# The output product of a decoder step: half of its features computed with the activations as TensorE weights

## What the kernel computes

```
y  = x + gate[:, None] * (u @ w_out)          # u: (tokens, 1024), w_out: (1024, 1024)
                                              # gate: one row of 1024 for the prompt, one for each of 8 samples
out = y * rsqrt(mean(y * y, axis=-1) + 1e-6) * final_g
```

## Time and profile before

| | |
|---|---|
| median of three runs | 756.62 us |
| the profiled execution | 757.0 us |
| its span, first to last instruction | 755.3 us |
| mean granted TensorE clock | 0.949 |
| TensorE matmul busy | 688.0 us, 91% |
| ScalarE, VectorE, GpSimd busy | 45%, 64%, 61% |

### The profile page before, as it was taken

The page is one execution under the profiler, slowest core; times in us unless marked ns, Lnnn a source line. Parts: engine busy times, 40 slices in busy tenths (PEclk is TensorE's granted clock), DMA queues, the critical chain, the costliest instruction groups (busy, mean ns, idle before and its releaser), DMA issues.

```text
span 755.3 us, 14932 instructions
## 1 busy us (share of the span) xinstructions
PE 688.0 (91%) x5066; PEld 618.9 (82%) x5066; DVE 482.8 (64%) x468; ACT 338.2 (45%) x760; POOL 464.3 (61%) x293
## 2 busy tenths in 40 slices
PE   2899999998988889999999999995899999999992
PEld 0576888786867858988999999985889998999992
DVE  0530589898988975895696597667665369343222
ACT  5634474646353335454463563530422225233554
POOL 4211266685756515898789679666594656666651
PEclk9898899999989979999999999999699999999996
DMA  8976858988788761277866768659247365832102
GB/s 315 336 253 220 243 174 249 272 252 271 237 269 265 215 207 29 87 237 208 250 199 185 216 208 241 182 177 240 56 122 212 97 181 154 266 85 83 57 0 113
DMA packets 156904, 144.71 MB, mean 192 GB/s; under 512 B 7547, under 2 KB 115152, under 8 KB 156852
## 3 DMA queue, kind: packets, MB, share of 16 engines
q1 hardware_dynamic: 142696, 136.10, 60.0%
q10 hardware_dynamic: 14164, 8.07, 3.4%
HBM read 135.10 MB, written 9.11 MB: 191 GB/s over the span
## 4 chain that ended last, share of the span: by engine, by line
PE 33%; issue 23%; POOL 20%; DVE 11%; SPq 6%; DMA 4%; ACT 1%; POOLq 0%; DVEq 0%; ACTq 0%
PE ps L545 26%; POOL sb_wL L1417 8%; POOL sb_arenaA L1491 8%; POOL sb_arenaA L1459 3%; DMA sb_arenaA<-in_w_ada 3%; DVE sb_arenaA L1728 2%; SPq L392 2%; SPq L393 2%; DVE sb_arenaA L1870 1%; PE ps L579 1%; DVE sb_arenaA L1875 1%; DVE sb_arenaB L1875 1%; DVE sb_arenaA L1732 1%; PE ps L653 1%; PE ps L900 1%
## 5 line engine op out<-in xcount | busy, mean ns | idle before, releaser
L1417 POOL TENSOR_TENSOR sb_wL<-sb_wraw,sb_wH 128x512 fp32r<-128x512 f32 (+1 forms) x176 | 236.3, 1359 | 200.0 <-ACT sb_wH L960 183.7
L545 PE MATMUL ps<-sb_hH,sb_wH 128*128 128x260 f32 x1152 | 241.6, 292 | 1.6 <-ACT sb_arenaB L965 0.9
L545 PE MATMUL ps<-sb_hL,sb_wH 128*128 128x260 f32 x1152 | 235.5, 287 | 0.0
L545 PE MATMUL ps<-sb_hH,sb_wL 128*128 128x260 f32 x1152 | 235.1, 286 | 0.0
L545 PEld LDWEIGHTS ps<-sb_hH,sb_wH 128*128 128x128 f32 x1152 | 181.7, 193 | 14.9 <-issue 10.6
L960 ACT ACTIVATE sb_wH<-sb_wraw 128x512 fp32r<-128x512 f32 (+1 forms) x176 | 104.1, 613 | 195.0 <-PE ps L545 158.6
L545 PEld LDWEIGHTS ps<-sb_hL,sb_wH 128*128 128x128 f32 x1152 | 181.6, 193 | 0.0
L545 PEld LDWEIGHTS ps<-sb_hH,sb_wL 128*128 128x128 f32 x1152 | 181.2, 192 | 0.0
L1491 POOL TENSOR_TENSOR sb_arenaA<-sb_arenaA 128x2048 f32<-128x2048 f32 x32 | 116.0, 3631 | 5.0 <-DMA sb_arenaA<-in_cache_v 3.0
L1732 DVE TENSOR_REDUCE sb_arenaA<-sb_arenaA 128x2048 f32 (+1 forms) x32 | 72.9, 2284 | 4.4 <-DVE sb_arenaA L1728 2.5
L1459 POOL TENSOR_TENSOR sb_arenaA<-sb_arenaA 128x2048 f32<-128x2048 f32 x11 | 54.3, 4939 | 29.5 <-DMA sb_arenaA<-in_cache_k 29.5
(11 more groups left out here) (356 smaller groups left out, 949.9 us busy)
## 6 DMA issues: line engine op xcount, KB each, us to landing
sb_wraw<-in_w_in SPq DMA_DIRECT2D x64, 512.0 KB, 5.2
sb_arenaA<-in_cache_k SPq DMA_DIRECT2D x128, 256.0 KB, 3.1
sb_arenaA<-in_cache_v SPq DMA_DIRECT2D x128, 256.0 KB, 3.3
sb_arenaA<-in_w_ada SPq DMA_DIRECT2D x6, 2048.0 KB, 12.4
sb_arenaB<-in_state_C SPq DMA_DIRECT2D x8, 512.0 KB, 3.9
sb_wraw<-in_w_mlstm SPq DMA_DIRECT2D x8, 512.0 KB, 4.4
sb_wraw<-in_w_out SPq DMA_DIRECT2D x8, 512.0 KB, 3.7
sb_arenaB<-in_x_prompt SPq DMA_DIRECT2D x1, 2048.0 KB
```

Source lines behind the costliest of these rows:

```text
L545: last = mm(ps[:, 2 * s + a, 0:HALF], w[:, s, k, :], x[:, k, a * HALF:(a + 1) * HALF], start=(k == 0 and w is wH and x is xH), stop=(k == ...
L1417: tt(wL[:, j % 2, part], wraw[:, j % 4, part], wH[:, j % 2, part].bitcast(F32), ALU.subtract)\
```

## The change

Tiles T_OUT to T_OUT + 3 (features 0 to 511) stay as they are, with their turns. Features 512 to 1023 of the prompt are computed the other way round. `hH` and `hL`, which are free once the `w_mlstm` product is done, take the high and low parts of w_out's last four tiles as 8 x 128 rows of 512 columns (`wide_high` on ScalarE, `wide_low` on VectorE). `out_tokens(i)` then uses 128 tokens of u as the stationary operand and streams 512 columns of w_out: 8 x 3 = 24 matmuls for a block of 128 tokens and 512 features, already in tokens by features, in PSUM bank i.

The gate is now along the columns, so it is needed as a row that all partitions hold (`alphaB`) and as 8 rows for the samples (`alphaS`). TensorE makes both ahead of the `w_mlstm` product and ScalarE copies them. VectorE multiplies the block in PSUM by `alphaB` and adds it to x (`added`). The samples' last 512 features come from eight small matmuls in plain float32 in four column groups (`uS`, 32 wide, with the raw w_out) and one that adds the groups. Squares, root, scaling and store are made for each token block by itself (`token_squares`, `deviation`, `finish`, `token_scale`): VectorE scales the second 512 features and ScalarE the first, and all five stores are issued from SP's queue.

```diff
@@ sync
-            for i, j in enumerate((0, 2)):
+            for i, what in enumerate((0, 1, None, 2, 3)):
                 sp.wait_ge(y_rdy, i + 1)
-                sp.dma_start(y_rows[:, j, :], yN[:, j, :]).then_inc(st_y, 16)
-            sp.wait_ge(y_rdy, 3)
-            sp.dma_start(O["y_s"].rearrange("b o d -> (b o) d"), ysN).then_inc(st_y, 16)
+                if what is None:
+                    sp.dma_start(O["y_s"].rearrange("b o d -> (b o) d"), ysN).then_inc(st_y, 16)
+                else:
+                    sp.wait_ge(y_act, what + 1)
+                    sp.dma_start(y_rows[:, what, :], yN[:, what, :]).then_inc(st_y, 16)
@@ tensor
             pe.wait_ge(ym_lo, 3)
+            pe.wait_ge(mod_rdy, 3)
+            pe.wait_ge(kq_used, 2 + 8)
+            for j in range(4):
+                mm(ps[:, 6, j * P:(j + 1) * P], modT[:, 20 + j, B:B + 1].broadcast_to([P, P]), ident[:, :],
+                   start=True, stop=True)
+            for j in range(4):
+                last = tr(ps[0:B, 7, j * P:(j + 1) * P], modT[:, 20 + j, 0:B], ident[:, :])
+            last.then_inc(fin_pe, 1)
...
+            out_turn(0, 0)
+            ztile(2, T_OUT + 2, uH, uL)
+            out_turn(1, 1)
+            ztile(3, T_OUT + 3, uH, uL)
+            out_turn(0, 2)
+
+            def out_tokens(i):
+                pe.wait_ge(z_free, T_OUT + (5 if i < 2 else 6))
+                for k in range(KT):
+                    for u, w in ((uH, hH), (uH, hL), (uL, hH)):
+                        last = mm(ps[:, i, :], u[:, k, i * P:(i + 1) * P], w[:, k, 0:D // 2],
+                                  start=(k == 0 and u is uH and w is hH), stop=(k == KT - 1 and u is uL))
+                last.then_inc(ot_mm, 1)
+
+            pe.wait_ge(kq_lo, 1 + 4)
+            out_tokens(0)
+            out_turn(1, 3)
+            pe.wait_ge(y_acc, 2 + 3)
+            for k in range(KT):
+                g = k % 4
+                last = mm(ps[32 * g:32 * g + 32, 4, :], uS[:, k, :], wraw[:, :, k, :], start=(k < 4), stop=(k >= 4))
+            last.then_inc(fin_pe, 1)
+            out_tokens(1)
+            pe.wait_ge(fin_act, 4)
+            mm(ps[0:B, 5, :], groupsum[:, 0:B], groups, start=True, stop=True).then_inc(ot_mm, 1)
+            out_tokens(2)
+            out_tokens(3)
@@ scalar
+            act.wait_ge(fin_pe, 2)
+            f(alphaB, ps[:, 6, :], ACT.Copy).then_inc(fin_act, 1)
+            f(alphaS, ps[0:B, 7, :], ACT.Copy).then_inc(fin_act, 1)
...
+            def wide_high(j):
+                act.wait_ge(ld_w[j % 4], 16 * (T_OUT // 4 + 2))
+                act.wait_ge(z_done, T_OUT + 2)
+                f(hH[:, :, (j - 4) * P:(j - 3) * P], wraw[:, j % 4], ACT.Copy).then_inc(ym_hi, 1)
...
+            def token_squares(i, acc):
+                act.wait_ge(y_acc, acc)
+                chain(f(osq[:, 0:D // 2], xN[:, i, D // 2:D], ACT.Square, accum_out=ssq[:, 4, i:i + 1]))
+
+            def token_scale(i, var):
+                act.wait_ge(y_var, var)
+                f(yN[:, i, 0:D // 2], yN[:, i, 0:D // 2], ACT.Copy, scale=ssq[:, 5, i:i + 1]).then_inc(y_act, 1)
...
@@ gpsimd
-            for j in range(8):
-                if j < 6:
-                    low(j + 2, T_OUT + j + 2)
-                if j >= 1:
-                    gained(j - 1)
-            gained(KT - 1)
+            for j in range(2):
+                low(j + 2, T_OUT + j + 2)
+            for j in range(4):
+                gained(j)
@@ vector
+            def wide_low(j):
+                dve.wait_ge(ym_hi, 2 + j - 3)
+                col = slice((j - 4) * P, (j - 3) * P)
+                tt(hL[:, :, col], wraw[:, j % 4], hH[:, :, col].bitcast(F32), ALU.subtract).then_inc(kq_lo, 1)
...
+            def added(x, acc, alpha, count):
+                dve.wait_ge(ot_mm, count)
+                chain(tt(acc, acc, alpha, ALU.mult))
+                tt(x[:, second], x[:, second], acc, ALU.add).then_inc(y_acc, 1)
+
+            def finish(i, number, std, whole=False):
+                rows = B if whole else P
+                x, y = (xs2, ysN) if whole else (xN[:, i], yN[:, i])
+                dve.wait_ge(y_acc, number)
+                chain(tt(y[:, second], x[:, second], fg[0:rows, second], ALU.mult))
+                dve.wait_ge(y_std, std)
+                v.reciprocal(ssq[0:rows, 5, i:i + 1], rstd[0:rows, i:i + 1]).then_inc(y_var, 1)
+                dve.wait_ge(y_var, 1 + std)
+                part = slice(0, D) if whole else second
+                v.tensor_scalar(y[:, part], y[:, part], ssq[0:rows, 5, i:i + 1], None, ALU.mult).then_inc(y_rdy, 1)
...
```

More of the change, by code:

```diff
@@ L1385, in _, with deviation @@
-            squares(KT - 1)
-            act.wait_ge(y_var, 1)
[L1387 to L1394, removed]
+            def deviation(i, rows):
+                f(rstd[0:rows, i:i + 1], ssq[0:rows, 4, i:i + 1], ACT.Sqrt, scale=1.0 / D, bias=ss[0:rows, i:i + 1])\
+                    .then_inc(y_std, 1)
@@ new lines, in token_squares @@
+            def token_squares(i, acc):
[4 more added lines that the diff above has]
+                f(yN[:, i, 0:D // 2], yN[:, i, 0:D // 2], ACT.Copy, scale=ssq[:, 5, i:i + 1]).then_inc(y_act, 1)
+            wide_high(4)
+            wide_high(5)
+            high(2, T_OUT + 2, T_OUT // 4)
+            out_leave(0)
@@ new lines, in _ @@
+            high(3, T_OUT + 3, T_OUT // 4)
+            out_leave(1)
+            squares(0)
+            wide_high(6)
+            out_leave(2)
+            wide_high(7)
+            squares(1)
+            out_leave(3)
+            squares(2)
+            token_squares(0, 6)
+            squares(3)
+            act.wait_ge(y_var, 1)
+            deviation(0, P)
+            act.wait_ge(y_gain, 4)
+            token_scale(0, 2)
+            act.wait_ge(fin_pe, 3)
+            f(groups, ps[:, 4, :], ACT.Copy).then_inc(fin_act, 1)
@@ L1396, in _ @@
+            token_squares(1, 8)
+            deviation(1, P)
+            token_scale(1, 3)
+            act.wait_ge(y_acc, 9)
+            chain(f(osq[0:B, 0:D // 2], xs2[:, D // 2:D], ACT.Square, accum_out=ssq[0:B, 4, 4:5]))
+            deviation(4, B)
+            for i in (2, 3):
+                token_squares(i, 8 + i)
+                deviation(i, P)
+                token_scale(i, 3 + i)
             act.wait_ge(st_misc, 16 * 6)
@@ L2062, in _ @@
             chain(v.memset(ssq, 0.0))
+            dve.wait_ge(uu_rdy, 1 + KT)
+            v.tensor_copy(uS[:, :, 0:B], sgm[:, :, T:NT])
             dve.wait_ge(ld_xo, 48)
[L2064 to L2070, removed]
@@ L2079, in _, with token_added @@
-            v.tensor_scalar(ysN, ysN, ss[0:B, 4:5], None, ALU.mult).then_inc(y_rdy, 1)
+            wide_low(4)
+            wide_low(5)
+            gated_sample(0)
+            turned(0, 1)
+            gated_sample(1)
+            wide_low(6)
+            turned(1, 2)
+            gated_sample(2)
+            wide_low(7)
+            turned(2, 3)
+            gated_sample(3)
+            dve.wait_ge(fin_act, 3)
+            def token_added(i, count):
+                added(xN[:, i], ps[:, i, :], alphaB, count)
@@ new lines, in _ @@
+            token_added(0, 4)
+            turned(3, 5)
+            dve.wait_ge(y_sq, 4)
+            chain(v.tensor_reduce(rstd[:, :], ssq[:, 0:4].rearrange("p c j -> p j c"), AX, ALU.add))
+            v.tensor_scalar(ss[:, :], rstd[:, :], 1.0 / D, EPS, ALU.mult, ALU.add).then_inc(y_var, 1)
+            finish(0, 6, 1)
+            token_added(1, 6)
+            finish(1, 8, 2)
+            added(xs2, ps[0:B, 5, :], alphaS, 7)
+            dve.wait_ge(y_gain, 4)
+            finish(4, 9, 3, True)
```

68 lines of the change are left out of this document (33 added, 35 removed).

## The result

The changed kernel takes 747.13 us (median of 9 runs, 743.70 to 750.10) against 756.16 us of the kernel before (9 runs, 750.60 to 757.75): a ratio of 0.9903, 95% interval 0.9876 to 0.9930, faster by 5.3 to 9.4 us. I forecast 751.5 us, in a range of 749.3 to 754.3.

The account below looks back on a forecast made before the run. TensorE, busy until 739.81 us, and a 15.5 us tail were taken to bound the kernel. TensorE +3.2 and tail -8.3 took 5.1 us off the span of 755.3; median forecast 751.5 us, range 749.3 to 754.3.

Parts of the forecast that it names:

- gate rows: TensorE ahead of the w_mlstm product: four matmuls and four transposes add 1.4 us, between 1.2 and 1.9.
- four tiles and three turns replaced: TensorE's w_out product: 24.6 us of tiles and turns become 26.4 us in the changed program, 1.8 more.
- tail: From the last product's end to the end of the span: from 15.5 to 7.2 us, -8.3.
- The level: Base of the forecast: profiled execution 757.0 us, 0.4 above the median of 756.62, less 5.1, gives a median of 751.5.
- 512-column streams at 0.235 us: Token blocks on TensorE: 96 matmuls at 0.235 us take 22.6 us, against 23.0 for the four tiles.
- The cheaper stream of 0.216: Rival: 512-column matmuls run at 0.216 us as in plain float32, giving 749.7 us; 8 in 100.
- The slower rival: Token blocks: weight loads not hidden under the 512-column stream; halfway, 9.6 us more, 761 us; 4 in 100.
- Changes of shape, 0.5 us: TensorE's w_out product: four changes of shape or operand cost 0.5 us in all, between 0 and 0.7.
- No helper late: Wide pieces and groups' copy come before TensorE wants them, thinnest cover 0.8 us; late-helper rival 1 to 3 us, 14 in 100.
- The tail's steps, 3.5 us to the last issue: Behind token block 3: gate product, addition, square, root, reciprocal and scaling take 3.5 us with gaps; last store issued at 746.5.
- The lone store: End of span: last 512 KB store takes 3.7 us from issue, bounds 3.3 and 5.8; long-store rival +2.1 us, 6 in 100.

Follow-up runs that it names:

- the one large store: Kernel before with only the last of its four 512 KB stores and the small one, three token blocks not written: stretch 117.72 us, tail 12.64 us.
- the held stores: Changed kernel with all five stores held back until the last token block is scaled: stretch 120.32 us, ratio to the kernel before 0.9984.
- before again: The kernel before run once more with no edit: median 755.41 us of 12 runs, ratio 1.0018 to the kernel before, stretch 120.53 us.

## Why the prediction was right and wrong

What a run can show step by step is the stretch. Forecast and measured, us:

| term | forecast | measured |
|---|---|---|
| gate rows | +1.4 | +1.03 (the edit alone, and its removal 1.0) |
| four tiles and three turns replaced | +1.8 | +1.36 |
| tail | -8.3 | -8.80 |
| sum | -5.1 | -6.4 |

- **The level.** The step that failed is the base of the forecast: "this execution lies 0.4 above the median of 756.62, so the forecast for the median is 751.5 us". I took three runs as the kernel's level and the range as that of the edit alone. Runs of one kernel spread over 6 to 11 us. Of the nine runs of the kernel before that stand beside the result, the three that I had are among the four slowest, and the other six have their median at 752.5; 35 later runs have theirs at 753.3, 13 at 753.8 and 12 at 755.4. My 1.5 us for what a measurement can tell from no change was too small as well: nine runs against nine left 2 us to either side. Taking the measured 6.4 us off 756.6 gives 750.2, inside the range; taking it off 753.3 gives 746.9, within 0.3 us of what was measured, and below the range. My own 5.1 off 753.3 would have been 748.2, also below. A miss of the level alone was enough for the time to leave the range, and the terms together moved it a further 1.3.
- **512-column streams at 0.235 us**: 0.2315, so 96 of them take 22.2 us and not 22.6, and the swap by itself gives 0.8 us against the four tiles' 23.0. The cheaper stream of 0.216, the rival for which the Trainium skill ("TensorE: Matmul & The Clock Gate", "Back-to-back issue gap") also stood, did not come; that section calls its formula the isolated gap and has 131 ns for 512 columns in a sustained stream, and no run here shows that either. The slower rival, weight loads that don't hide, did not come: 48 loads instead of 24 a block cost 0.1 us.
- **Changes of shape, 0.5 us**: about that. Blocks, turn and samples add up to 26.0 us from 709.30 to 735.30, against 26.4. Without the streams' 22.2, the turn's 0.55, the samples' 1.85 and the sum of the groups' 0.96 some 0.4 us are left for the changes and for the end of the last matmul.
- **The gate rows**: they take 0.92 + 0.44 = 1.36 us, as I said, but part of that was a gap before: TensorE stood 0.2 us at the start of the w_mlstm product, and the first new instruction fills it. How the rest of the 0.3 splits was not tried.
- **No helper late**: right, TensorE does not wait once in the w_out product. The copy of the groups ended at 721.98 us, 1.0 ahead of its use (I said 0.8).
- **The tail's steps, 3.5 us to the last issue**: 3.6. The root took 0.29 instead of 0.21 and the square was exact.
- **The lone store**: 3.7 us allowed, 3.0 measured from SP's queue and 3.4 from ScalarE's. This term was mis-sized by 0.7, the largest error in the sum of the edit. "to landing" in the earlier trace rows counts from the issue for loads and stores of other shapes, and I put 0.3 on top of it.
- **What the tail was made of**: I read it as squares. Ahead of the prediction I even counted 16 of 128 columns behind the last product; the trace has eight, of tiles 6 and 7, and one of the samples for each. Leaving them out was worth 1.4 us; behind them stood GpSimd's product with `final_g`, with which VectorE's next step collides. The change took both away, since that product of the last half now runs on VectorE beside ScalarE's square. The tail's sum came out nearly right all the same, since I priced the new steps one by one; the cause of the old ones I had only half seen. The stores' queueing was 2.4 us and an issue between two scalings 0.4 (shown by the one large store), and the issues on one queue are another 2.6 that a changed kernel without the early stores would have paid (shown by the held stores).

The profiles differ by another 6.9 us ahead of the product of squares. Over all twelve profiles it lies between 627.7 and 635.1 us, both of these in a kernel with one small edit in its last part, and the two kernels' own four stand at 634.7 and 630.9, 627.8 and 630.4. By the order of VectorE's operations nearly all of the difference between the first two profiles arises between 226 and 287 us, where the sums over cached pages end and the choice of blocks is made. The largest step in it is one addition: ahead of it the changed kernel leads by 2.2 us, behind it by 6.6. Before:

```profile
237.30 4.59 POOL L1459 TENSOR_TENSOR sb_arenaA<-sb_arenaA 128x2048 f32<-128x2048 f32 x1 [4.58 <-DMA sb_arenaA<-in_cache_k]
237.34 6.70 DVE L1728 TENSOR_TENSOR sb_arenaA<-sb_arenaA 128x2048 f32<-128x2048 f32 x1
```

After:

```profile
235.13 2.28 DVE L1800 TENSOR_TENSOR sb_arenaA<-sb_arenaA 128x2048 f32<-128x2048 f32 x1
235.26 6.64 POOL L1533 TENSOR_TENSOR sb_arenaA<-sb_arenaA 128x2048 f32<-128x2048 f32 x1 [4.70 <-DMA sb_arenaA<-in_cache_k]
```

Two additions of 2048 columns meet. The one that starts second, VectorE's by 0.04 us or GpSimd's by 0.13, takes 4.4 us longer or 2.1. It is the collision of the kernel's tail again, and an order settled by a tenth of a microsecond moves VectorE by 4.4 us. Six of the twelve profiles, with edits of either kernel among them, have VectorE's addition long at this place (5.2 to 6.7 us instead of 2.28). It is not the whole of the scatter: the lead is down to 5.0 us at 254 us and back to 7.1 at 287, two other profiles, the latest of all among them, have such an addition at 195 us instead, and what settles the order was not tried. The fall of TensorE's clock behind the wait for VectorE, seen in two of twelve profiles at 1.2 to 1.5 us each, is a second, smaller source. In the timed runs, too, a slower one tends to have the lower mean granted clock (before again: 751.32 us at 0.962, 760.30 at 0.947); which of the two follows from the other was not tried.

## What to carry to other kernels

When TensorE is busy to the end, swapping which operand is stationary gives it little (0.8 us here, less than the gate rows and the samples cost); what pays is that a product's last piece leaves in the layout and the portion in which it can be finished and stored, so that norm, scaling and stores of all other pieces run beside TensorE. Price a tail by everything in it: the late engine, the one right behind it, the issues in one queue and the bytes in flight. And before a range is given, ask how far runs of the same kernel spread: a change of under 1% is read from a stretch of the trace between two fixed instructions. Here it repeated to 0.01 us, except where the granted clock fell in it, while the median of three runs was 3 us off.

## What the runs showed of the hardware beyond this

- A 512-column fp32r matmul costs 0.2315 us at full clock and a 256-column one 0.118: 0.44 ns a column and about 5 ns fixed. A pass of plain float32 comes to 0.216 us for 512 columns, so the fp32r form costs more for each pass.
- A VectorE operation of 5 columns took 1.60 instead of 0.17 us and one of 8 columns 0.68 instead of 0.15, each ending with a GpSimd operation with two SBUF inputs. Of two additions of 2048 columns that met, the second to start took 6.6 to 6.7 us.
- The last 512 KB store by itself is done 3.0 to 3.4 us behind its issue, and five issues in a row on SP's queue are 2.6 us from the first to the last.
